# The first normalization through a diagonal on TensorE, and residue order for the dilated keys

## What is computed

```python
mod = silu(c) @ ada_w + ada_b
shift1, scale1, gate1, shift2, scale2, gate2 = split(mod, 6)
h = rmsnorm(x, norm1_w) * (1 + scale1) + shift1
gq, gk, gv, gr, g_lr, aq, ak, av, merge_a, merge_b = split(h @ w_in)
# dilated attention: 3 groups of 4 heads, (window, dilation) = (128, 1), (512, 4), (2048, 16)
q, k = rotary(aq, positions), rotary(ak, positions)
# a query of a group attends to keys of its own residue modulo the dilation
```

## Time and profile before

| | us |
|---|---|
| median of 3 runs | 995.71 (994.65 to 998.25) |
| the profiled execution | 996.0 |
| its span, first to last instruction | 994.2 |
| TensorE busy | 950.3 (96%) |
| VectorE busy | 517.7 (52%) |
| ScalarE busy | 373.3 (38%) |
| GpSimd busy | 94.8 (10%) |
| mean granted TensorE clock | 0.961 of full speed |

### The profile page before, as it was taken

One profiled execution on the slowest core, in us unless ns is written; L12 is line 12 of the kernel. 1 busy time (PEld: TensorE's weight loads), 2 busy tenths in 40 slices (PEclk: granted clock), 3 DMA queues, 4 the chain that ended last, 5 costly groups with the idle time before them and its releaser, 6 DMA issues.

```text
span 994.2 us, 11999 instructions
## 1 busy us (share of the span) xinstructions
PE 950.3 (96%) x4659; PEld 795.7 (80%) x4659; DVE 517.7 (52%) x643; ACT 373.3 (38%) x457; POOL 94.8 (10%) x66
## 2 busy tenths in 40 slices
PE   3689999999999999999999997999999999999997
PEld 2589888778898888888888885888888888888885
DVE  4994673554584636463343435654555556533223
ACT  4362111526743434544322323433343343332225
POOL 4720421100000000000002223000000000000003
PEclk9699987979999999999999999999999999999999
DMA  9826744422433212122222441334333432322302
GB/s 336 332 97 191 226 150 125 149 85 85 169 123 90 85 44 79 50 85 85 85 85 85 160 137 43 85 84 117 94 84 96 115 84 85 127 85 84 121 5 85
DMA packets 114015, 112.68 MB, mean 113 GB/s; under 512 B 4516, under 2 KB 104230, under 8 KB 111671
## 3 DMA queue, kind: packets, MB, share of 16 engines
q1 hardware_dynamic: 113255, 109.96, 34.8%
q10 hardware_dynamic: 720, 2.16, 0.6%
HBM read 104.77 MB, written 4.19 MB: 110 GB/s over the span
## 4 chain that ended last, share of the span: by engine, by line
PE 92%; DVE 5%; issue 1%; DMA 1%; ACT 0%; SPq 0%; DVEq 0%; ACTq 0%
PE bank L1478 26%; PE bank L1480 26%; PE bank L1479 26%; DVE ada_in L957 3%; PE bank L1693 2%; PE bank L1603 2%; DMA ada_in<-in_ada_w_dram 1%; PE bank L1872 1%; PE bank L1575 1%; PE bank L1680 1%; PE bank L1639 1%; PE bank L1714 1%; PE bank L1598 1%; PE bank L1614 1%; DVE h_lo L1406 1%
## 5 line engine op out<-in xcount | busy, mean ns | idle before, releaser
L1478 PE MATMUL bank<-h_hi,w_hi 128*128 128x512 f32 (+1 forms) x696 | 279.2, 401 | 1.4 <-DVE rope_t L1048 0.8
L1479 PE MATMUL bank<-h_lo,w_hi 128*128 128x512 f32 (+1 forms) x696 | 273.7, 393 | 0.0
L1480 PE MATMUL bank<-h_hi,w_lo 128*128 128x512 f32 (+1 forms) x696 | 273.7, 393 | 0.0
L1478 PEld LDWEIGHTS bank<-h_hi,w_hi 128*128 128x128 f32 (+1 forms) x696 | 131.7, 189 | 30.0 <-issue 1.9
L1480 PEld LDWEIGHTS bank<-h_hi,w_lo 128*128 128x128 f32 (+1 forms) x696 | 131.6, 189 | 28.8
L1479 PEld LDWEIGHTS bank<-h_lo,w_hi 128*128 128x128 f32 (+1 forms) x696 | 131.6, 189 | 27.3 <-issue 0.2
L991 DVE TENSOR_TENSOR w_lo<-raw,w_hi 128x2048 fp32r<-128x2048 f32 (+3 forms) x48 | 88.2, 1849 | 63.2 <-ACT w_hi L564 63.2
L998 DVE TENSOR_TENSOR w_lo<-raw,w_hi 128x2048 fp32r<-128x2048 f32 x32 | 73.4, 2293 | 91.7 <-ACT w_hi L572 91.7
L564 ACT ACTIVATE w_hi<-raw 128x2048 fp32r<-128x2048 f32 (+2 forms) x45 | 73.4, 1644 | 76.3 <-DMA raw<-in_w_in_dram 67.4
L1432 DVE SCALAR_TENSOR_TENSOR conv<-bank,vecs,conv 128x511 f32<-128x511 f32 x88 | 65.7, 748 | 67.5 <-ACT conv L886 62.0
L572 ACT ACTIVATE w_hi<-raw 128x2048 fp32r<-128x2048 f32 x33 | 62.9, 1905 | 72.2 <-PE bank L1480 72.2
(11 more groups left out here) (235 smaller groups left out, 1361.3 us busy)
## 6 DMA issues: line engine op xcount, KB each, us to landing
raw<-in_w_up_dram SPq DMA_DIRECT2D x44, 512.0 KB, 4.6
raw<-in_w_in_dram SPq DMA_DIRECT2D x19, 1024.0 KB, 5.3
raw<-in_ada_w_dram SPq DMA_DIRECT2D x16, 1024.0 KB, 5.5
raw<-in_w_down_dram SPq DMA_DIRECT2D x22, 512.0 KB, 3.9
raw<-in_w_in_dram SPq DMA_DIRECT2D x20, 512.0 KB, 5.2
ada_in<-in_ada_w_dram SPq DMA_DIRECT2D x16, 512.0 KB, 8.0
raw<-in_w_gla_branch_dram SPq DMA_DIRECT2D x4, 1024.0 KB, 4.9
raw<-in_w_out_dram SPq DMA_DIRECT2D x4, 1024.0 KB, 5.1
```

Source lines behind the costliest of these rows:

```text
L1478: pe.matmul(out_ap, wh, xh, start=first, stop=False, skip_group_check=True)
L1479: pe.matmul(out_ap, wh, xl, start=False, stop=False, skip_group_check=True)
L1480: return pe.matmul(out_ap, wl, xh, start=False, stop=last, skip_group_check=True)
```

## The change

**The head.** VectorE squares and sums x in token layout (`sum_squares`, one fused instruction for a block of 128 tokens, its elementwise output dropped into `h_lo`). ScalarE makes four inverse roots per partition, and from them four diagonal matrices (`diag`, in the space of `ada_acc`). TensorE multiplies each 128x128 block of `x_tok` with the diagonal in place of the identity, which gives the normalized tile; ScalarE copies it to `xn_tile(k)`. The transposes with the identity stay, for the spill. `modulated` and `lower` then work from `xn_tile`; for k = 6 and 7 the unrounded value comes from VectorE (`modulate_late`). GpSimd has no part left in the head but the memsets of `v_ext`, which now wait for `xn_ps` and the spill only.

For j = 0 and 1, rows 3 and 7 of the adaptive weights go straight to TensorE with silu(c) as column, and the two sums are added there too: four groups of four column products in place of one. The first rows of j = 2 and 3 are ScalarE's.

TensorE's order is written anew: high parts of the first product as tiles come (`first_hi`), the first half of the wide values (`wide_hi`) between them, the low parts behind the last column product, then `wide_rest`. The load of the second weight unit moves ahead of that of adaptive part 2.

**Residue order.** `rotate` writes tiles of groups 1 and 2 in residue order, reading bank and `cs` at a step of four elements; the scores then read contiguous tokens.

```diff
             for j in range(KT // 2):
-                if j == 1:
-                    load(0)
+                if j in (1, 2):
+                    load(j - 1)
                 load_first(j)
...
-            pool.wait_ge(xt_ps, KT)
-            pool.wait_ge(hl_done, KT // 2)
+            pool.wait_ge(xn_ps, KT)
             pool.wait_ge(spilled, 16)
...
             for k in range(KT):
                 act.wait_ge(xt_ps, k + 1)
-                square(0, k, sq, bank[3 + k % 4][:, :])
                 act.activation(xT0[:, k, :], bank[3 + k % 4][:, :], ACT.Copy).then_inc(xt_sb, 1)
             act.preload_act_table_set(LN_EXP)
+            act.wait_ge(ssq_done, NB)
+            act.activation(stat[:, NB:2 * NB], stat[:, 0:NB], ACT.Ln, scale=1.0 / D, bias=EPS).then_inc(tok_ln, 1)
+            act.wait_ge(tok_ln, 1)
+            act.activation(stat[:, NB:2 * NB], stat[:, NB:2 * NB], ACT.Exp, scale=-0.5).then_inc(tok_rstd, 1)
+            act.wait_ge(tok_rstd, 1)
+            act.wait_ge(ident_in, 16)
+            for b in range(NB):
+                act.activation(diag[:, b, :], cst[:, C_ID:C_ID + P], ACT.Copy,
+                               scale=stat[:, NB + b:NB + b + 1]).then_inc(diag_done, 1)
+            for k in range(KT):
+                act.wait_ge(xn_ps, k + 1)
+                act.activation(xn_tile(k), bank[3 + k % 4][:, :], ACT.Copy).then_inc(xn_sb, 1)
+            act.wait_ge(xn_sb, KT)
             split_hi(0)
-            inverse_root(0, rstd[:, :], bank[0][:, :])
-            for k in range(KT):
-                if k == 0:
-                    ada_first_rows(2)
+            modulated(0)
+            modulated(1)
+            split_hi(1)
+            modulated(2)
+            modulated(3)
+            ada_first_rows(2)
+            ada_first_rows(3)
+            for k in range(4, KT):
                 modulated(k)
-                if k == 5:
-                    split_hi(1)
...
+            def sum_squares(b):
+
+                dve.wait_ge(x_in[b], 16)
+                dve.tensor_tensor_reduce(h_lo[:, 2 * b:2 * b + 2, :].rearrange("p a n -> p (a n)"), x_tok[:, b, :],
+                                         x_tok[:, b, :], 1.0, 0.0, ALU.mult, ALU.add,
+                                         stat[:, b:b + 1]).then_inc(ssq_done, 1)
...
+            def modulate_late(k):
+
+                dve.wait_ge(hl_done, k - NT_ACT + 1)
+                dve.wait_ge(gain_done, k // 2 + 1)
+                dve.tensor_scalar(xn_tile(k - NT_ACT), xn_tile(k), gain[:, 0, k:k + 1], mod[:, k:k + 1],
+                                  ALU.mult, ALU.add).then_inc(nt_late, 1)
...
-                dve.tensor_tensor(rope[:, j % 2, t, :], src[:, :], cs[:, 0, :], ALU.mult)
-                free(tile, dve.tensor_tensor(rope_t[:, 1 - t, :], src[:, :], cs[:, 1, :], ALU.mult))
+                own, other = rope[:, j % 2, t, :], rope_t[:, 1 - t, :]
+                src, cos, sin = src[:, :], cs[:, 0, :], cs[:, 1, :]
+                if g > 0:
+                    own, other = (v.rearrange("p (r l) -> p r l", r=DIL) for v in (own, other))
+                    src, cos, sin = (v.rearrange("p (l r) -> p r l", r=DIL) for v in (src, cos, sin))
+                dve.tensor_tensor(own, src, cos, ALU.mult)
+                free(tile, dve.tensor_tensor(other, src, sin, ALU.mult))
...
-            for j in range(2):
-                for half in range(2):
-                    ada_sums(j, half)
+            for b in range(NB):
+                sum_squares(b)
+            ada_sums(0, 0)
+            ada_sums(0, 1)
             shift_and_gain(0)
             split_lo(0)
+            ada_sums(1, 0)
+            ada_sums(1, 1)
             shift_and_gain(1)
+            split_lo(1)
+            lower(0)
+            lower(1)
             ada_sums(2, 0)
             ada_sums(2, 1)
+            shift_and_gain(2)
+            lower(2)
+            lower(3)
             ada_sums(3, 0)
-            shift_and_gain(2)
             ada_sums(3, 1)
-            for k in (4, 5):
+            shift_and_gain(3)
+            for k in range(NT_ACT, KT):
+                modulate_late(k)
+            for k in range(4, KT):
                 lower(k)
-            shift_and_gain(3)
-            split_lo(1)
-            for k in (6, 7):
-                lower(k)
...
+            for k in range(KT):
+                if k < 4:
+                    pe.wait_ge(xt_sb, k + 5)
+                else:
+                    pe.wait_ge(xn_sb, k - 3)
+                for b in range(NB):
+                    if k == 0:
+                        pe.wait_ge(diag_done, b + 1)
+                    last = pe.matmul(bank[3 + k % 4][:, b * P:(b + 1) * P], x_tok[:, b, k * P:(k + 1) * P], diag[:, b, :],
+                                     start=True, stop=True, skip_group_check=True)
+                last.then_inc(xn_ps, 1)
...
+                if j < 2:
+                    pe.wait_ge(silu_done, 1)
+                    pe.wait_ge(ones_set, 1)
+                    for half, k in enumerate(DIRECT):
+                        pe.wait_ge(ada_landed[2 * j + half], 32)
+                        columns(ada_rows(j, k), c_silu[:, k:k + 1], half == 0, False)
+                    for half in range(2):
+                        pe.wait_ge(ada_step, 6 * j + 5 + half)
+                        last = columns(ada_rows(j, half), ones[:, 0:1], False, half == 1)
+                else:
+                    pe.wait_ge(ada_sum, j - 1)
+                    last = columns(ada_rows(j, 0), ones[:, 0:1], True, True)
                 last.then_inc(mod1_ps, 1)
...
                         for r in range(DIL):
-                            tok = slice(r, SEQ, DIL)
+                            tok = slice(r * P, (r + 1) * P)
...
             shift_scale(0)
+            first_hi(0)
+            first_hi(1)
+            shift_scale(1)
+            first_hi(2)
+            first_hi(3)
+            wide_hi(0)
+            wide_hi(1)
+            shift_scale(2)
+            wide_hi(2)
+            wide_hi(3)
+            first_hi(4)
+            first_hi(5)
+            shift_scale(3)
+            for k in range(KT // 2):
+                first_lo(k)
+            for k in range(KT // 2):
+                wide_lo(k)
+            first_hi(6)
+            first_hi(7)
+            for k in range(KT // 2, KT):
+                first_lo(k)
...
-            for half in range(2):
-                wide_values(half)
+            wide_rest()
```

More of the change, by code:

```diff
@@ L576, in square @@
                     act.wait_ge(sum_done, SUMS[part] + k - 1)
-                if k < 2 and part > 1:
+                if k < 2 and part > 0:
                     act.wait_ge(ssq_ps, part)
@@ L969, in shift_and_gain @@
                 dve.wait_ge(vec_sb, 1)
-                dve.tensor_tensor(mod_v[:, :, two], bank[7 - j % 2][:, 0:4].rearrange("p (s k) -> p s k", s=2),
+                dve.tensor_tensor(mod_v[:, :, two], bank[7][:, 4 * j:4 * j + 4].rearrange("p (s k) -> p s k", s=2),
                                   bias_v[:, :, two], ALU.add).then_inc(mod_done, 1)
@@ L1011, in modulate @@
                 if k == 0:
+                    if r == 0:
+                        dve.wait_ge(xn_ps, KT)
                     if r == 1:
@@ L1554, in product @@
                 last.then_inc(acc_ready, 1)
-            def wide_values(half):
-                n = UNIT[("vw", half, 0)]
-                pe.wait_ge(raw_used, RAW_AT[("w", n)] + 1)
-                for r in range(NB):
-                    for j in range(KT // 2):
-                        k = half * KT // 2 + j
-                        w = tuple(v[:, n % 2, 2 * j * UW:2 * (j + 1) * UW] for v in (w_hi, w_lo))
-                        s = tuple(v[:, k, r::DIL] for v in (h_hi, h_lo))
-                        last = three(side[1 + r][:, :], s, w, k == 0, k == KT - 1)
-                    if half == 1:
-                        last.then_inc(vw_ready, 1)
-                if half == 0:
-                    last.then_inc(vw_half, 1)
             def ada_part(r, k):
@@ L1749, in gla, with first_hi @@
                               skip_group_check=True).then_inc(gssq_ps, 1)
-            shift_scale(0)
-            pe.wait_ge(sum_done, SUMS[0] + KT - 1)
-            pe.matmul(bank[0][:, :], ones[:, :], sq_sum[:, :], start=True, stop=False)
-            pe.wait_ge(sq_done, KT)
-            pe.matmul(bank[0][:, :], ones[:, :], sq[:, (KT - 1) % 2, :], start=False, stop=True).then_inc(ssq_ps, 1)
-            shift_scale(1)
-            pe.wait_ge(raw_used, 1)
-            pe.wait_ge(rstd_done, 1)
-            for k in range(KT):
-                if k in (2, 5):
-                    shift_scale(2 + k // 4)
-                w = [v[:, 0, k * UW:(k + 1) * UW] for v in (w_hi, w_lo)]
+            def first_hi(k):
+                if k == 0:
+                    pe.wait_ge(raw_used, 1)
                 pe.wait_ge(hh_done, k + 1)
@@ L1865, in _ @@
             for k in range(KT):
```

(2 more changed lines are left out.)

185 lines of the change are left out of this document (101 added, 84 removed).

## The result

The changed kernel takes 985.45 us (median of 4 runs, 983.68 to 989.03) against 996.74 (4 runs of the kernel before, 994.65 to 998.25): ratio 0.9893, 95% interval 0.9858 to 0.9928. The profiled execution took 989.03 us, the slowest of the four; its span is 987.3.

What follows compares the result with a forecast made beforehand. VectorE was taken to bound the head, until about 63 us, and TensorE everything behind it. Head +0.2, scores -8.3, rotate +1.6 and clock -3.1 make -9.6 from 995.7: 986 us, range 975 to 996.

Steps and rivals of the forecast that it cites:

- The head, +0.2: Start to first query-key pass: VectorE's gain is given back by queue order, 86.3 against 86.1, +0.2 us.
- TensorE's last columns 40.0; gain 40.4: Head, j=1: after VectorE's sums end at 38.7, TensorE's column products end at 40.0 us and the gain at 40.4.
- the checkpoint: Start of the first query-key pass, where both kernels' heads are compared: 86.14 us before, 86.3 forecast.
- The memset, +1: Head, GpSimd's `v_ext` memsets beside VectorE's j=2 work: they slow VectorE by 1 us, bounds 0 and 3.7.
- The scores, -8.3: Score products of groups 1 and 2: contiguous operands save 0.130 us on each of 64 passes, -8.3 us.
- rival D: Score products: residue order saves nothing because something other than the stride sets 0.242 us; total 994, chance 0.04.
- Rotate, +1.6: VectorE's strided rotates in the query-key units: +1.0 us a tile, +1.6 us on the path, bounds 0 and +4.
- clock, -3.1: Dense passes behind the scores: the first two falls of the granted clock vanish, -3.1 us, bounds 0 and -8.4.
- the third fall: Low clock at 214.5 to 228.2 us, with a TensorE wait and products of 17 rows: taken as untouched by the change.
- B's first half: Rival for the head: diagonal and column products at the low clock, +9 us; whole rival 994, chance 0.17.
- A: Rival: the head shortens too, passes at the high clock and memsets free, about -5 more; 980, chance 0.13.
- C: Rival: TensorE stays at the low clock from diagonal products to wide values, +27 us; total 1013, chance 0.08.

Runs made afterwards that it cites:

- the mended kernel: Changed kernel with column products earlier, VectorE's sums before `split_lo(0)`, `wide_lo` later, and ScalarE copying rotary factors into residue order for step-free reads: 970.82 us.
- the last kernel: The mended kernel with VectorE's split of the third weight unit put ahead of the last two operations of the rotary angles: 961.86 us.

## Why the prediction was right, and where it wasn't

The total was right, 986 against 985.45, with a range that held, but that it fits so well is luck. Two terms of the sum were too favourable by some 3 us each, the head and the rotate, and a gain of 6 us that it didn't have, from the shift of the addresses, made up for both. By its own signs the first query-key pass at 89.9 lies outside the 86 give or take 3 that it called right.

**The head, +0.2.** Most steps came within 1.2 us: diagonal passes to 28.0 (29.2 forecast), first gain 31.7 (32.9), the wait of 5.0 (4.8) and the low clock behind it. The step that failed is "TensorE's last columns 40.0; gain 40.4": it counted one group of column products behind VectorE's sums of j=1. TensorE, in its own order, first ran 16 passes of `first_hi` that had begun only at 34.1, for `h_hi` from ScalarE, and then all 32 columns at the low clock: 6.9 us, gain at 44.8, though VectorE's sums were done at 37.5, 1.2 us ahead of the forecast. That gain is 4.4 us later than forecast, the fourth 3.9, the checkpoint 3.6; against the kernel before, the head costs 3.8 us in the profile and some 3 by the runs. The prediction had a price for the fillers at the low clock (24 us), but asked only whether they fit in the gaps, not what they do to the column products queued behind them. With both orders changed (`shift_scale` on TensorE, `split_lo(0)` on VectorE) the checkpoint is at 78.3. A slip has no effect: 58.3 and 9.5 us make 67.8, not 67.4, and the wait went on to 72.4 in any case.

**The memset, +1 (bounds 0 and 3.7).** It cost 0: the two subtractions beside the memsets took 1.29 us, as they do at 54.84 without one, and the six multiply-adds, of which the memsets met the first 1.3 us, took 4.07, as at 56.05. The Trainium skill (SBUF — State Buffer, section "Who interferes with whom") had said so: a VectorE instruction with two SBUF inputs doesn't contend with a GpSimd instruction that only writes. The slow conversion of the earlier trace rows, 3.01 us, takes 0.43 now that no memset runs beside it; the row next to the memset told of another kind of operation.

**The scores, -8.3.** Measured 16.4 to 8.3 us busy, and 3.86 to 1.79 for sixteen. Right, and rival D is out.

**Rotate, +1.6, and clock, -3.1.** The runs give -7.0 for residue order, with a wide interval, and the profiles of the stage some -7 on average, where these two and the scores make -9.8. The operation was over-priced (0.37 added, not 0.5), its effect under-priced, and this is the second term that failed: with the step of `cs` gone and nothing else changed, the stage is 6.5 us shorter in the profile (188.1 to 181.6), and 3.5 in the mended kernel (184.8 to 181.3). The prediction counted the split for one unit and 1.0 us at the last query-key tile, and followed the delay no further. The chain shows what is late next: VectorE's products release GpSimd's two rotations (4.5 us), these SyncE's shuffles, and only behind them in SyncE's queue is the load of the next weights issued (134.57). Its split is done at 146.2, and only then come VectorE's copies of S and its next rotations. TensorE waits 2.5 us ahead of the last query-key tile instead of 0.8, and the low clock around that place lasts 6.8 us longer.

The falls at 143 and 204 did vanish as forecast. All five profiles with strided scores have both; of the nine with residue order one has a fall of 3.4 us near the first. The longer stretch about cancels their 3.1, and it goes with the step: with contiguous `cs` it is back at 13.7. Without the step the stage is 11.5 us shorter than before, about the scores' 8.3 and the clock's 3.1 together. That is not a clean account, since the third fall, which the prediction left alone, also shrank, from 13.7 us in the five to 10.2 or 6.8 in the nine; no run prices it by itself.

The Trainium skill (SBUF — State Buffer, section "Door 1: The DMA port swizzle") says that an access which crosses to a new line pays, and of PSUM's 8-byte lines that non-contiguous access slows matmuls. The prediction read this as a rule for VectorE's reads of PSUM as well. Here VectorE reads the bank at that step in 0.69 us, so for that reading the measurement decides against it, and for the SBUF operand (+0.37 us) it agrees.

**The shift, not in the sum.** Shown from both sides: 6.2 us from an unused tensor, 390 against 395 ns, and back again without `stat`. The prediction took all code behind 279 us as unchanged; the diff's line that declares `stat` changed its addresses.

**Rivals.** B's first half came partly (a longer head, from the column products at the low clock), A not in this kernel; a shorter head came only with the changed orders, 976. C did not come: TensorE was at the low clock from 33 to 50 us, then back at 1.00, and had its fillers done at 60.

## What to carry to other kernels

An engine's queue is part of the cost of an item: when a product that others wait for is put behind fillers, price the fillers at the low clock as well, and let the short product that releases an engine go first. When a stride is moved from one engine to another, follow the releases on to the next load in the DMA queue, and test which operand carries the cost. When the time of a stage changes though none of its lines did, compare the same group's mean duration in both traces, and test the addresses with an unused tensor before you explain the rest.

## What the runs showed of the hardware

- A shift of the tensors that TensorE reads as moving operands by 128 bytes, from 896 to 1024 bytes past a multiple of 1024, changes fp32 passes of 512 columns from 395 to 390 ns, here 6.2 us in all. Shifts of 384 and 640 bytes give 390 as well.
- VectorE's product of a bank with SBUF takes 0.69 us with a 16-byte step in the bank alone and 1.06 with one in both, for 128x512 fp32. The SBUF operand's step costs all of it.
- Fp32 score products of 128 columns take 0.112 us a pass with contiguous operands and 0.242 at a step of 16 bytes.
- A fused square and sum of 128x1024 fp32 takes 1.22 us and 0.08 for the accumulator.
- In or right behind the pause of 5.0 us ahead of `wide_rest`, the granted clock fell to 0.50 (1.2 GHz) for 3.4 to 6.8 us in all five profiles that have it; behind one of 2.7 us for 3.4 us in two profiles and not at all in a third; behind one of 1.2 us it did not fall. The six runs of the last kernel differ by 12 us, with mean granted clocks from 0.988 to 0.973.
